# Delta rule stage: four chains of one 128-token tile instead of two chains of two, and a new issue order on TensorE

## What is computed

```python
# per head and direction; s is a 64 x 64 state
def step(s, inp):                       # r, w, k, v, a, b of one token
    sa = einsum('bhvk,bhk->bhv', s, a)
    s = s * w + sa * b + v * k          # outer products
    y = einsum('bhvk,bhk->bhv', s, r)
    return s, y
y  = ys[0] + ys[1]                      # both directions
yn = (y - mean(y)) * rsqrt(var(y) + eps) * lnx_g + lnx_b
out = (yn + bonus) * gate
```

## Time and profile before

| | us |
|---|---|
| median of 3 runs | 3956.01 |
| lowest and highest of them | 3952.75, 3965.37 |
| span of the profiled execution | 3941.6 |
| of it the stage, first issue of its loads to first issue of the next stage | 771.72 to 1358.74 = 587.0 |
| TensorE busy over 781 to 1359 us | 441.6 |
| VectorE, ScalarE, GpSimd busy there | 316.1, 135.2, 224.3 |

### The profile page before, as it was taken

The page is one execution under the profiler, slowest core; times in us unless marked ns, Lnnn a source line. Parts: engine busy times, 40 slices in busy tenths (PEclk is TensorE's granted clock), DMA queues, the critical chain, the costliest instruction groups (busy, mean ns, idle before and its releaser), DMA issues. The chain is left out here.

```text
span 3941.6 us, 97846 instructions
## 1 busy us (share of the span) xinstructions
PE 3377.2 (86%) x38463; PEld 2331.6 (59%) x38463; DVE 2360.6 (60%) x4245; ACT 1768.8 (45%) x2361; POOL 731.1 (19%) x706
## 2 busy tenths in 40 slices
PE   4999799677778587979998998999689999878789
PEld 0899788577677475733332333333267777666567
DVE  1688688655555466627776766776377574056631
ACT  0577577422222124307776766776222321156620
POOL 4000000043444200331221221222112333200000
PEclk7999899899899788989999999999899999988899
DMA  8354445421221255949889999953734323265452
GB/s 315 84 171 139 160 130 166 159 86 46 61 72 44 82 167 200 209 155 315 277 263 356 351 354 357 326 160 76 244 87 128 86 75 96 95 153 132 117 181 75
DMA packets 520291, 665.36 MB, mean 169 GB/s; under 512 B 77168, under 2 KB 423984, under 8 KB 516768
## 3 DMA queue, kind: packets, MB, share of 16 engines
q1 hardware_dynamic: 494576, 572.44, 45.2%
q0 software_dynamic: 25216, 86.62, 8.9%
q10 hardware_dynamic: 48, 0.05, 0.0%
HBM read 493.08 MB, written 165.94 MB: 167 GB/s over the span
## 5 line engine op out<-in xcount | busy, mean ns | idle before, releaser
L2600 PE MATMUL routed_p_gu<-routed_fixed,routed_x 128*32 128x512 f32 x3840 | 572.5, 600 | 0.0
L2600 PE MATMUL routed_p_gu<-moe_exp_w,routed_x 128*32 x1280 | 571.5, 600 | 0.7 <-DVE routed_fixed L2722 0.7
L2654 ACT COPY routed_fixed<-moe_exp_w 128x1024 f32 x320 | 332.6, 1047 | 222.1 <-DMA moe_exp_w<-in_exp_w_up_dram 86.3
L2722 DVE COPY routed_fixed<-moe_exp_w 128x1024 f32 x640 | 398.0, 681 | 51.3 <-DMA moe_exp_w<-in_exp_w_up_dram 42.9
L544 PE MATMUL front_ps<-front_a_high,front_w_high 128*128 128x320 f32 (+1 forms) x1120 | 362.7, 324 | 16.3 <-DVE front_w_low L797 13.4
L544 PE MATMUL front_ps<-front_a_low,front_w_high 128*128 128x320 f32 (+1 forms) x1120 | 353.8, 316 | 0.0
L544 PE MATMUL front_ps<-front_a_high,front_w_low 128*128 128x320 f32 (+1 forms) x1120 | 353.7, 316 | 0.0
L2600 PEld LDWEIGHTS routed_p_gu<-moe_exp_w,routed_x 128*32 128x32 f32 x1280 | 135.4, 111 | 356.2 <-issue 356.2
L3606 PE MATMUL pre_ps<-pre_a_high,pre_w_high 128*128 128x512 f32 x720 | 287.1, 399 | 13.3 <-ACT pre_xb L3753 6.7
L2615 PE MATMUL routed_p_y<-routed_wd,routed_hT 128*32 x640 | 290.4, 597 | 3.4 <-ACT routed_fixed L2665 3.4
L2615 PE MATMUL routed_p_y<-routed_fixed,routed_hT 128*32 128x512 f32 x1920 | 291.4, 597 | 0.0
(11 more groups left out here) (550 smaller groups left out, 7386.6 us busy)
## 6 DMA issues: line engine op xcount, KB each, us to landing
moe_exp_w<-in_exp_w_gate_dram SPq DMA_DIRECT2D x64, 1024.0 KB, 13.3
moe_exp_w<-in_exp_w_up_dram SPq DMA_DIRECT2D x64, 1024.0 KB, 16.4
routed_wd<-in_exp_w_down_dram SPq DMA_DIRECT2D x64, 1024.0 KB, 15.1
front_wt<-in_w_in_dram SPq DMA_DIRECT2D x70, 512.0 KB, 4.4
mod_w<-in_w_mod_dram SPq DMA_DIRECT2D x24, 1024.0 KB, 18.2
pre_wt<-in_w_in_dram SPq DMA_DIRECT2D x44, 512.0 KB, 4.0
out_a<-mix SPq DMA_DIRECT2D x24, 512.0 KB, 4.0
total<-out_none SPq DMA_DIRECT2D x24, 512.0 KB
```

The lines of the kernel that those rows point to most:

```text
L2600: op = nc.tensor.matmul(p_gu[spot(s), :], x[:, b % 2, k, spot(s)], w, start=(k == 0), stop=(k == KD - 1))
L2654: nc.scalar.copy(fixed[:, place_of(b, c), 0, :], wgu[:, bass.ds(e % WS, 1), c * D:(c + 1) * D].rearrange("p o n -> p (o n)"))\
L2722: op = nc.vector.tensor_copy(fixed[:, place_of(b, c), s - 1, :], wgu[:, bass.ds(es[s] % WS, 1), c * D:(c + 1) * D].rearrange("p o n -> p ( ...
```

## The change

`rwkv_mix` is rewritten; `two_blocks` now keeps `a, r, b, k` in one tensor and `bonus, gate` in another (views of it carry the old names). What differs:

- **Four chains** (u = 0 to 3, `GROUPS = QT`), each for 128 channels with 2 PSUM banks, `OFFSET = 5`. A chain runs through 10 tiles; a tile is 8 problems. A product is 8 matmuls, half as many as before, and each eviction is half as wide.
- **Slots of a tile:** `turn, lay, prod, masked, t0`, then `w1, t1` to `w5, t5`, then `as0, vn0, st0, as1, vn1, st1`: 21, numbered 0 to 20. The norm's eight slots are put between them in tiles 7 to 9 and follow the last tile. In all 242 slots, and 257 rounds with the offsets.
- **Fewer products:** the transposed inverse comes from two transposes per level (L1190) instead of 16 matmuls; `wup`, `mn`, `intra`, `query` and the `c` slots are replaced by two steps per tile, each of three dependent products: `as` (queries A times the state, L1266), `vn` (T times what VectorE made of it, L1273) and `st` (the state's new part, L1196). The outputs are made in the whole array (L1202) and from the states (L1278).
- **ScalarE** now puts `bk` and `uv` into stacked layouts by copies of half the partitions (L1299), two in `turn` and four in `lay`. `prod` waits for `lay`.
- **GpSimd** also multiplies the state by its decay (`faded0`, `faded1`, L1464); VectorE's new state waits for that. `turn` of a tile waits for VectorE's `y` (or `st1`) of the tile before.
- **The order on TensorE:** in each round first the parts in the whole array (or with 128 rows) of all chains, function `whole`, then the parts in quarters of all chains, function `quarters`.
- **Loads:** ten per tile and chain; those that `once` counts (`tot`, `lnx`) are issued after the first 40, and VectorE, ScalarE and GpSimd wait for them.

```diff
-    PAIRS = TILES // 2
-    UNITS = 2 * PAIRS
+    GROUPS = QT
...
-    OFFSET = 11
+    OFFSET = 5
...
-            for s in range(len(order) + OFFSET):
-                for u in range(2):
-                    if 0 <= s - OFFSET * u < len(order):
+            for s in range(len(order) + OFFSET * (GROUPS - 1)):
+                for body in bodies:
+                    for u in range(GROUPS):
+                        if 0 <= s - OFFSET * u < len(order):
...
+        def freed(eng, n, u):
+
+            if n >= 0:
+                DV.wait(eng, by_vector[u], n, "y" if latent(n) else "st1")
...
+            for u in range(GROUPS):
+                load(0, u)
+            for d in range(2):
+                sp.dma_start(tot[:, :, d, :], rw["tot"][d].rearrange("(u p) c -> p u c", p=P)).then_inc(once, 16)
...
+            def whole(n, p, u, b):
...
+                if p == "turn":
+                    pe.wait_ge(loaded[u][z], (n // 2 + 1) * (16 * LOADS))
+                    freed(pe, n - 1, u)
...
+                elif p == "t0":
+                    DV.wait(pe, by_vector[u], n, "cc")
+                    PO.wait(pe, by_pool[u], n, "tt")
...
+                elif p[0] == "w" and p != "w1":
+                    l = int(p[1])
+                    AC.wait(pe, by_scalar[u], n, "res" if l == 4 and finishing(n) else f"t{l - 1}")
+                    for e in range(2):
+                        nc.tensor.transpose(b[:, 0, span(TT_AT + e * P, P)], T[u][:, 2 * e:2 * e + 2, :], consts["ident"][:, :])
...
+            def quarters(n, p, u, b):
...
+                if p == "prod":
+                    AC.wait(pe, by_scalar[u], n, "lay")
...
+            interleaved(whole, quarters)
...
+                if p == "turn":
+                    PE.wait(act, products[u], n, p)
+                    stack(bk, 0, 0, 0).then_inc(by_scalar[u], 1)
+                elif p == "lay":
+                    stack(bk, 1, 0, 1)
+                    stack(uv, 1, 2 * P, 1).then_inc(by_scalar[u], 1)
...
+                elif p[:2] == "st":
+                    s = int(p[2])
+                    PE.wait(dve, products[u], n, p)
+                    if s == 0 or n < LAST:
+                        PO.wait(dve, by_pool[u], n, f"faded{s}")
...
+                if p == "prod":
+                    DV.wait(pool, by_vector[u], n, "at")
+                    PE.wait(pool, products[u], n - 1, f"t{LEVELS}")
+                    for h in range(2):
+                        for c in range(2):
+                            first_level(c, h)
+                    pool.drain()
+                    nc.gpsimd.tensor_tensor(TT[u][:].rearrange("p e c t -> p (e c) t"), TT[u][:].rearrange("p e c t -> p (e c) t"), eye4, ALU.add)\
+                        .then_inc(by_pool[u], 1)
+                    for l in range(1, 4):
+                        level(l)
```

More of the change, by code:

```diff
@@ L1026, in slots, with finishing @@
+        def finishing(n):
+            return second(n - 1)
         def slots(n):
-            out = ["turn", "prodb", "prodk", "zed", "t0"]
+            norm = ["mean", "square", "var", "root", "norm", "back", "res", "gate"] if finishing(n) else []
+            if n == TILES:
+                return norm
+            out = ["turn", "lay", "prod", "masked", "t0"] + norm[0:1]
             for l in range(1, LEVELS + 1):
-                out += [f"w{l}", f"t{l}"]
-            out += ["wup", "mn"] + (["intra"] if latent(n) else []) + ["c0"] + (["query"] if latent(n) else []) + ["c1", "c2"]
@@ L1031, in slots @@
-            out += ["c3"] if not last(n) else []
-            out += ["inter"] if latent(n) else []
-            out += ["mean", "square", "var", "root", "norm", "back", "gate"] if last(n) else []
-            return out
+                out += [f"w{l}"] + norm[2 * l - 1:2 * l] + [f"t{l}"] + norm[2 * l:2 * l + 1]
+            return out + ["as0", "vn0", "st0", "as1", "vn1"] + (["st1"] if latent(n) or n < LAST else [])
         def pe_steps(n):
-            out = ["ta", "tb", "tk", "tv", "prodb", "prodk", "zed", "t0"]
+            back = ["back"] if finishing(n) else []
@@ L1075, in first_tile @@
[L1075 to L1089 removed]
+            norm = ["square", "root", "res"] if finishing(n) else []
@@ new lines, in act_steps @@
+            if n == TILES:
+                return norm
+            out = ["turn", "lay", "t0"]
+            for l in range(1, LEVELS + 1):
+                out += ([f"tt{l}"] if l > 1 else []) + (norm[l - 1:l] if l < 3 else []) + [f"t{l}"] + (norm[2:3] if l == 3 else [])
+            return out + ["vn0", "vn1"]
+        def pool_steps(n):
+            gate = ["gate"] if finishing(n) else []
+            if n == TILES:
+                return gate
+            return ["tt"] + [f"x{l}" for l in range(1, LEVELS + 1)] + gate + ["faded0"] + (["faded1"] if n < LAST else [])
@@ new lines, in heads, with product, strict @@
+                    return ap.rearrange("p h e v -> p (h e) v")
+                def product(rows, c, side):
+                    v = b[rows, :, span(2 * P * c, 2 * P)].rearrange("p h (e j t) -> p h e j t", e=2, j=2)
+                    return v[:, :, :, side, :]
+                def strict(out, other):
+                    for c in range(2):
+                        rows = half(1 - c if other else c)
+                        op = nc.vector.tensor_tensor(out[u][rows].rearrange("p (e h) t -> p h e t", h=2), product(rows, c, 0),
+                                                     mask(MASK_AFTER)[rows].rearrange("p e h t -> p h e t"), ALU.mult)
+                    op.then_inc(by_vector[u], 1)
```

665 lines of the change are left out of this document (298 added, 367 removed).

## The result

| | before | changed |
|---|---|---|
| median, us | 3954.38 (4 runs, 3948.32 to 3965.37) | 4120.25 (4 runs, 4116.86 to 4126.78) |
| span of the profiled execution | 3941.6 | 4124.8 |
| stage, first issue to the next stage's first issue | 587.0 | 775.78 to 1531.79 = 756.0 |
| TensorE's granted clock in the stage | 0.94 | 0.78 |

The ratio is 1.0428, 95% interval 1.040 to 1.0456: 166 us slower, where 97 were forecast. In the profiled executions the stage is 169 us longer.

A forecast was written before the change was run, and what follows sets the result against it. No engine's sum but the chain of waits through the rounds bounds the stage: 24 + 44 + 532 + 36 + 28 + 6 = 670, plus 14, 684 us against 587.0, so 3956 + 97, about 4053 us; range 3925 to 4165.

The forecast's parts named there:

- GpSimd's block: GpSimd's TT (3.0 us) and X levels (2.1 us) before `faded1`: about 5 us, the most frequent cause of waits.
- first eviction: ScalarE's start in the stage: `once` waits for the 44th issue plus 2 us, so 24 us after 771.7, near 795.
- No engine's sum decides: Whole stage: TensorE about 340 us, ScalarE 326, GpSimd 315, VectorE 281, none near the stage's time; round length decides.
- well under 70%: TensorE's busy share of the stage, forecast to be well under 70%.
- tile 0: First tile of the stage, without states to wait for: four stretches of 11 us, 44 us.
- half of the instruction waits: TensorE's instruction waits: 28 us for some 12,000 instructions, half of them on the chain, 14 us.
- the stretch: Five rounds from one chain's `turn` to the next's: 15.1 us, 13.8 where chain 0 turns; 59.1 us a tile.
- `lay` done at 5.6 us: ScalarE's `lay` copies, queued behind three copies for the chain ahead's `t1` and `zed` ending at 4.5 us, end at 5.6.
- `prod` and the masks: TensorE's `prod` from 6.5 to 7.6 us, VectorE's `at` ending at 8.46, then GpSimd's TT ready at 11.5.
- What is late behind TT: After TT at 11.5 us: X until 13.6, `faded1` 14.2, VectorE's state and `y` 15.05, next `turn` 15.1.
- The clock: Rival 3: TensorE's idleness lowers its clock, doubling 3.2 us of streaming a stretch: 128 us more, 4180 us; chance 0.13.
- rival 1: Chains get past each other: stretch of 11.5 us, median 3938 us, about 3910 with GpSimd's cheap end; chance 0.17.

The follow-up runs named there:

- e2: Changed kernel with ScalarE instead of GpSimd multiplying the state by its decay (`faded0`, `faded1`): 4120.03 us, ratio 1.0428.
- e18: Changed kernel with 8 extra matmuls, results unused, in each `t0` slot before the wait for TT: 4106.54 us, ratio 1.0395.
- by-chain order: Changed kernel with TensorE issuing, each round, one chain's whole-array part and then its quarters, then the next chain's: 4032.18 us, ratio 1.0204.
- e20: Changed kernel in by-chain order, identity added by VectorE, `faded` on ScalarE, X levels 1 to 3 later, `lay` copies split between ScalarE and VectorE: 3943.25 us, ratio 0.9974.

## Why the prediction was right in sign and 67 us short

The time lies in the range given, near its slow end.

**Sign, place, most of the mechanism: right.** Nothing shows a change outside the stage; a `t0` that waits for GpSimd's TT at the head of its round is the largest wait; L1299 releases L1227 (7 us in eleven waits, besides the 17.8 at the start); GpSimd's block takes 5.1 us (1154.54 to 1159.68) and had been put at 3.0 + 2.1. The first eviction starts at 799.20 for "near 795":

```profile
799.20 1.51 ACT L1299 COPY rwmix_bk<-rwmix_ps 64x256 f32<-64x256 f32 x4 [37.94 <-DMA rwmix_lnx<-in_rw_lnx_b_dram]
```

The stage had started 4 us later, so this term held (23.4 us for 24). "No engine's sum decides" held as well. Two of the signs came out otherwise: TensorE isn't busy for well under 70% but for 68, since the low clock stretches its work; and GpSimd's block is the largest cause of waits by time (79.8 us) but not by number (37; the T copies 66).

**Which term was mis-sized.** By the turns, the 670 us of the sum and what they measured:

| term | forecast | measured |
|---|---|---|
| start to first eviction | 24 | 23.4 |
| tile 0, to chain 0's second `turn` (852.9) | 44 | 53.7 |
| 35 stretches (517) and 16 rounds of norm slots (24), to the last `turn` (1464.3) | 541 | 611.4 |
| last stretch, last rounds, norm, store | 61 | 67.5 |
| half of the instruction waits | 14 | no "issue" among the waits |
| stage | 684 | 756.0 |

The term is the stretch: 70 us of the 72 missing lie there. The other rows cancel: tile 0 and the end took 16 us more, the instruction waits 14 less. Two of the 35 stretches, with norm slots, took 31 us each; the other 33 took 16.6 on average, for 14.8 forecast. Within a stretch:

1. *`lay` done at 5.6 us*: 6.19. I gave ScalarE's second of two copies in a row 0.26 us, from 512-element rows that overlapped. That held behind a copy of 128 partitions (T at 1149.51, the next at 1149.78), but the copies of 64 partitions and 256 elements follow each other after 0.38 us and take 0.74 us a pair. Of 1.5 us for `lay` 0.4 were missing; the T copy behind it ends at 6.59 for 5.9, and `prod` starts at 7.29 for 6.5.
2. *`prod` and the masks*: from `prod`'s start to TT 5.0 us forecast, 5.25 in the stretch above, 5.58 on average. `prod` ran at the 1.2 GHz level in part of the stretches; its instructions took 0.42 us there instead of 0.28.
3. *What is late behind TT*: the wrong step. I let S wait for `faded1` and start 0.07 us behind it. In the stretch shown it waited for another chain's W: `t0`, `st1`, `w1` on TensorE, then TT copy, W, S. TT to `turn` was 4.75 us there and 4.32 on average, not 3.6. e2 shows that `faded1` didn't matter: without GpSimd's `faded` the time stays. In two of the twelve stretches, both opened by chain 0, it was as forecast. `faded1` came 1.2 us before the step that decided, so the wrong step cost the forecast little: that is luck.
4. *The clock*: I had made it a rival of its own with 128 us and said that "a part of it is likely in any case", but put no part of it into the sum. 0.78 over the stage is between. The part that filler at this one place gives back is 14 us (e18); the clock was still 0.89 there for 0.94 before, so the whole part may be larger.

**Not asked.** I priced the order only by its mode changes (32 to 64 us of TensorE off the chain) and followed the delays of the heads without asking what the other order would give. The order is worth 88 us of the 166: in the by-chain order this kernel would have been 78 us slower, and I would have counted its heads the same way. The sum of rival 1 has a slip: 428 us in place of 532 makes the stage 580 us and the median 3949, not 3938, which is inside the range that I had called "same". Rival 1 (chains get past each other, 11.5 us a stretch) was wrong for this order, but by chain, with the waits shortened, e20 comes to 12.4 us. I had put the point from which it decides at 12.1; e20 beats the kernel before with 12.4.

## What to carry to other kernels

Where several chains share queues of a fixed order, the order in a round sets how long each eviction may take. Here it paid to keep all of a chain's work for one slot together, so that the other chains' work always lies between two of its steps. Grouping by kind saves mode changes, which did not decide here, and puts the late ones at the head, ahead of everything that is ready. When such a chain is followed, do so for each engine's queue down to the step that really starts last, and try one relief at a time: the same relief (`faded` off GpSimd) gave 0 us in one order and was part of 54 us in the other.

## What the runs showed of the hardware that was not expected

- The idle time just before `t0` alone doesn't tell the level of the work behind it: L1202 took 1.07 us after 1.86 us without work (1157.78) and 0.64 us after 1.87 (1090.57), and by chain, after 1.22 us, it took 0.64 us mostly and 1.07 at times. With filler in the gap (e18) it was 0.64 in 24 of 26 cases.
- ScalarE's copy of 64 partitions by 256 elements takes 0.37 us, as long as one of 128 partitions by 256 elements (0.37), and four of them follow each other after 0.38 us where the next copy starts 0.27 us after one of 128 partitions did; why, no run shows. Cutting by partitions saves nothing; sharing by partitions between two engines brought `prod` 0.7 us forward.
- GpSimd's four drained operations on 64 partitions by 128 elements take 2.23 us, three of 128 by 256 2.09.
